# Router logits of a two-layer encoder trunk, made with the router's 36 columns stationary and turned back by two transposes

## The reference

```
g_logits = t @ w_group + b_group            # 256 tokens x 4 groups
e_logits = t @ w_expert + b_expert          # 256 tokens x 32 experts
p_group, g_sel = softmax(g_logits), argmax(g_logits)      # top 1 of 4 groups
top_v, top_i = top_k(e_logits of the chosen group, 2)     # top 2 of its 8 experts
gates = softmax(top_v) * p_group[g_sel], spread over the 32 experts
out = sum_e gates_e * (silu(t @ w1_e) * (t @ w3_e)) @ w2_e
```

## Time and profile before

| what | value |
|---|---|
| median of 3 runs | 1806.16 us |
| lowest, highest | 1806.05, 1807.55 us |
| profiled execution: first to last instruction (span) | 1807.0 us |
| mean granted TensorE clock of it | 0.953 |
| PE busy | 1640.9 us (91%) |
| PEld busy | 1163.6 us (64%) |
| DVE, ACT, POOL busy | 733.5 (41%), 414.5 (23%), 57.5 us (3%) |
| DMA | 543.77 MB, mean 301 GB/s |
| MATMUL psum_T<-router_w,xT | 128 records, 17.5 us busy |

### The profile page before, as it was taken

The page is one execution under the profiler, slowest core; times in us unless marked ns, Lnnn a source line. Parts: engine busy times, 40 slices in busy tenths (PEclk is TensorE's granted clock), DMA queues, the critical chain, the costliest instruction groups (busy, mean ns, idle before and its releaser), DMA issues.

```text
span 1807.0 us, 25442 instructions
## 1 busy us (share of the span) xinstructions
PE 1640.9 (91%) x9809; PEld 1163.6 (64%) x9809; DVE 733.5 (41%) x1154; ACT 414.5 (23%) x559; POOL 57.5 (3%) x82
## 2 busy tenths in 40 slices
PE   7999999998997998789789999999989887998785
PEld 7999998887552455345287988988855552455341
DVE  5545444443322232232264756757343222232233
ACT  5343343441000000000154334333310000000001
POOL 4010000100000000000011000000000000000000
PEclk9999999998999999999899999999989999999997
DMA  8545455457899999999944465464669999999996
GB/s 267 187 160 167 162 162 169 157 210 286 339 423 425 427 425 425 425 427 425 412 170 140 144 206 176 151 208 163 248 272 418 423 424 426 426 425 425 425 427 262
DMA packets 149418, 543.77 MB, mean 301 GB/s; under 512 B 8736, under 2 KB 25456, under 8 KB 116208
## 3 DMA queue, kind: packets, MB, share of 16 engines
q1 hardware_dynamic: 148448, 541.14, 77.0%
q0 software_dynamic: 912, 1.82, 0.4%
HBM read 540.83 MB, written 2.10 MB: 300 GB/s over the span
## 4 chain that ended last, share of the span: by engine, by line
PE 58%; issue 27%; DMA 9%; DVE 2%; ACT 1%; SPq 1%; DVEq 0%; POOLq 0%; POOL 0%; ACTq 0%
PE psum_G L662 33%; PE psum_S L662 16%; DMA ring<-in_moe_w 9%; PE psum_A L662 5%; PE psum_T L662 3%; DVE w_lo L406 1%; SPq L507 1%; ACT w_hi L402 1%; DMA x<-in_x 0%; PE psum_A L669 0%; DVE x L1580 0%; ACT squares L1122 0%; POOLq L598 0%; DVE h L1815 0%; PE psum_T L881 0%
## 5 line engine op out<-in xcount | busy, mean ns | idle before, releaser
L406 DVE TENSOR_TENSOR w_lo<-ring,w_hi 128x2048 fp32r<-128x2048 f32 x126 | 289.2, 2298 | 288.9 <-ACT w_hi L402 284.7
L662 PE MATMUL psum_A<-ring,arena 128*32 128x512 f32 x1984 | 272.8, 684 | 107.0 <-DMA ring<-in_moe_w 105.3
L402 ACT CAST w_hi<-ring 128x2048 fp32r<-128x2048 f32 x128 | 244.1, 1907 | 244.4 <-PE psum_G L662 155.9
L662 PEld LDWEIGHTS psum_A<-ring,arena 128*32 128x32 f32 x1984 | 65.1, 117 | 264.7 <-issue 264.6
L662 PE MATMUL psum_G<-arena_two,h 128*128 (+1 forms) x1024 | 230.8, 385 | 0.2
L662 PEld LDWEIGHTS psum_G<-arena_two,h 128*128 128x128 f32 x1024 | 225.8, 311 | 0.4 <-DVEq L1591 0.4
L1698 DVE COPY arena_two<-psum_A 128x512 f32<-128x512 f32 x64 | 44.3, 692 | 290.9 <-PE psum_A L662 290.5
L1728 DVE TENSOR_TENSOR x<-x,psum_S 128x512 f32<-128x512 f32 x128 | 88.1, 688 | 161.7 <-PE psum_S L662 161.7
L662 PE MATMUL psum_G<-xT_hi,w_hi 128*128 128x256 f32 x512 | 148.8, 291 | 0.9 <-DVE w_lo L406 0.6
L662 PE MATMUL psum_G<-xT_hi,w_lo 128*128 128x256 f32 x512 | 144.8, 283 | 0.0
L662 PE MATMUL psum_G<-xT_lo,w_hi 128*128 128x256 f32 x512 | 144.7, 283 | 0.0
(11 more groups left out here) (224 smaller groups left out, 2087.8 us busy)
## 6 DMA issues: line engine op xcount, KB each, us to landing
ring<-in_moe_w SPq DMA_DIRECT2D x376, 1024.0 KB, 17.2
ring<-in_sb_w_in SPq DMA_DIRECT2D x48, 1024.0 KB, 5.0
ring<-in_ml_w_in SPq DMA_DIRECT2D x48, 1024.0 KB, 5.1
ring<-in_sb_w_out SPq DMA_DIRECT2D x16, 1024.0 KB, 4.9
ring<-in_ml_w_out SPq DMA_DIRECT2D x16, 1024.0 KB, 5.0
extra_one<-in_moe_w SPq DMA_DIRECT2D x4, 1024.0 KB, 8.0
extra_two<-in_moe_w SPq DMA_DIRECT2D x4, 1024.0 KB, 13.6
x<-in_x SPq DMA_DIRECT2D x2, 1024.0 KB, 5.9
```

The costliest lines, as they stand in the source:

```text
L402: act.copy(w_hi[:, slot_place(j), :], ring[:, slot_place(j), :]).then_inc(hi_made, 1)
L406: dve.tensor_tensor(w_lo[:, slot_place(j), :], ring[:, slot_place(j), :], w_hi[:, slot_place(j), :].bitcast(F32), ALU.subtract).then_inc(l ...
L662: return pe.matmul(dst, lhsT, rhs, start=start, stop=stop, skip_group_check=True)
```

## The change

The operands of the logits' matmuls change places. For each tile k one f32 matmul takes the 36 columns of `router_w` as stationary operand and both token blocks of `xT`, 256 columns, as the moving one. The result is turned: 36 x 256 in T0, 36 logits on the partitions. Behind the last one PE waits until DVE has copied T0 to the new tile `logits_t` (a view of the arena) and then turns the two halves back with two transposes into bank T1, where it lies as it lay in T0 before. DVE's route starts with that copy, signals it, and waits for `filled["T1"]` instead of `filled["T0"]`. SP's two extra loads still wait for `filled["T0"]`. The table of bank uses counts one more use of T1 in each layer.

```diff
-        phase(("norm_ffn", layer), A=XC, T0=1)
+        phase(("norm_ffn", layer), A=XC, T0=1, T1=1)
...
+        logits_t = r(T)[0:ROUTER]
...
                     for k in range(4 * c, 4 * c + 4):
-                        for b in range(TB):
-
-                            last = mm(psum["T0"][:, b * ROUTER:(b + 1) * ROUTER], xT[:, k, b * P:(b + 1) * P],
-                                      router_w[:, k, :], k == 0 and b == 0, k == KT - 1)
+                        last = mm(psum["T0"][0:ROUTER, 0:T], router_w[:, k, :], xT[:, k, :], k == 0, k == KT - 1)
                     if c == XC - 1:
                         last.then_inc(filled["T0"], 1)
+                        pe.wait_ge(emptied["T0"], base["T0"] + 1)
+                        claim("T1", base["T1"])
+                        for b in range(TB):
+                            last = pe.transpose(psum["T1"][:, b * ROUTER:(b + 1) * ROUTER], logits_t[:, b * P:(b + 1) * P],
+                                                ident[0:ROUTER, 0:ROUTER])
+                        last.then_inc(filled["T1"], 1)
...
                 dve.wait_ge(filled["T0"], first_use["norm_ffn", layer]["T0"] + 1)
+                dve.tensor_copy(logits_t, psum["T0"][0:ROUTER, 0:T])
+                dve.drain().then_inc(emptied["T0"], 1)
+                dve.wait_ge(filled["T1"], first_use["norm_ffn", layer]["T1"] + 1)
                 for b in range(TB):
-                    last = dve.scalar_tensor_tensor(out=logits[:, b, :], in0=psum["T0"][:, b * ROUTER:(b + 1) * ROUTER],
+                    last = dve.scalar_tensor_tensor(out=logits[:, b, :], in0=psum["T1"][:, b * ROUTER:(b + 1) * ROUTER],
                                                     scalar=rstd[:, b:b + 1], in1=router_b[:, :],
                                                     op0=ALU.mult, op1=ALU.add)
-                last.then_inc(emptied["T0"], 1)
+                last.then_inc(emptied["T1"], 1)
```

## The result

The changed kernel takes 1809.59 us (median of 20 runs, 1808.7 to 1810.37) against 1807.24 us for the kernel before (20 runs on the same chip, 1805.9 to 1808.35). The ratio is 1.0013 [1.0007, 1.0019], or +2.35 us [1.3, 3.4]. The forecast was +2.5 us and 1808.7 us. So the sum came out, and it was no change by the mark of 0.2%. It came out by luck: three of its terms were mis-sized, and their errors cancel. That is what the rest is about.

The account below looks back on a forecast made before the run. PE bounds the out stages, the weight stream the experts, and the router's stretch delays that stream; +0.12 + 0.05 + 2.36 = +2.5 us on 1806.16 gives 1808.7 us, own range 1807.3 to 1809.9, 8 in 10 from 1805.4 to 1810.8.

Parts of the forecast that it names:

- The path: Between last logits matmul and mask, each lost microsecond restarts SP's weight stream a microsecond later, one for one, both layers.
- The logits steps inside the projection: Three steps a layer: half as many records, each twice as long, +0.02 us a step, +0.12 us for six.
- The rival that loads are not hidden: Every load in the logits steps stands between two matmuls: up to 0.114 us a record, 1816.0 us; chance 0.04.
- The fp32r pace: Rival: 256 f32 columns move as fast as fp32r ones, 0.115 us a logits record, 1800.6 us; chance 0.04.
- The rule of the Trainium skill that was weighed there: A load overlaps running matmuls only when its row group differs; the prediction said its trace disagrees.
- The last logits step: Step before the route, mostly at half clock: 3.61 us in layer 0, 2.75 in layer 1; +0.05 us for both.
- the rival that the clock holds: 256-column stream keeps PE at full clock in the last logits step: 1.89 us a layer, sum -0.7 us; chance 0.07.
- The handoff: After the last logits: DVE copy, drain, two half-clock transposes, return to DVE; 1.18 us a layer, 2.36 for both.
- its predicted lower bound of 0.87: Handoff with both transposes at full clock: 0.87 us a layer.
- The sum: +0.12 for steps inside the projection, +0.05 for last steps, +2.36 for handoffs: +2.5 us, 1808.7 us.
- The gap of 1.2 us to the bias: Sign: 1.2 us in place of 0.04 between the last logits matmul's end and DVE's first bias instruction.
- The restart of SP 1.2 to 1.4 us later in layer 0: Sign: mask, gather and SP's first issue of the next chunk come 1.2 to 1.4 us later than before.

Follow-up runs that it names:

- warm_route: Kernel before, plus unread 432-column f32 matmuls in PE's waits: one before the last turn, one before the last logits, seven before the count matmuls; 1805.43 us, ratio 0.9990.
- before_again: The kernel before, unchanged, run once more for a second profile; 1809.56 us.
- handoff_only: Kernel before with its old logits, plus only DVE's copy and PE's two transposes, their result unread; 1809.67 us, ratio 1.0013.
- grouped: Changed kernel with logits steps 0, 1 and 2 run together at the place of step 2; 1808.16 us, ratio 1.0007 of the kernel before.

## Why the prediction came out, and which of its steps failed

**The path.** Right. In layer 0 SP's queue restarts 21.2 us behind the count matmuls in all eleven profiles without unread matmuls (20.5 in warm_route, where they ran at a held clock). In layer 1 it is 21.2 us too, but 22.9 in before_again, handoff_only and grouped, where the first up projection was slow (below). The pause of 0 GB/s stays, and handoff_only shows two handoffs of 1.06 to 1.09 us as +2.35 us [0.7, 4.0] of time.

**The logits steps inside the projection, +0.02 us each.** This term was mis-sized. The pace was right: records 0.22 us apart, for 0.215 from the earlier trace rows. What was left out is the entry and the exit: with a narrow f32 operand the load is not taken ahead, and a step costs 0.25 to 0.27 us more. The earlier trace rows could not show it, since both of its operands have 128 columns. The last turn began 0.76 us later in layer 0, so six steps cost about +1.5 us, not +0.12. The rival that loads are not hidden was priced on each record and is wrong as such (there is no gap inside a step); it holds at the two ends of a step. The fp32r pace is refuted. Counting from the first logits record to the next projection matmul, as the earlier trace rows do, hides the entry; the count has to start at the last matmul ahead of it. The rule of the Trainium skill that was weighed there (TensorE: Matmul & The Clock Gate, section Packing small matmuls) fails here as well, as it was put there: loads for the same rows do overlap running matmuls, inside a step and, with 128 columns, at its start. The same section also has loads for a background weight buffer pulled ahead; these rows do not speak against that.

**The last logits step, +0.05 us for both layers.** Failed in size and in its reason. It takes 1.89 us in both layers: the rival that the clock holds, given 0.07, is what happened, to the hundredth of its 1.89. The argument against it was that in layer 0 the clock fell 0.07 us into the step, so the step had no say. That was a reading of one execution as if the place were fixed. Other executions of the same form fall 0.7 to 2.6 us into it, and the price of the old form is thereby an average: 2.4 us a step, not the 3.51 and 2.80 of the profile. Against 2.4 the new step gains 0.5 us a layer, about 1.0 us in all. So the rival had the step right and its own sum wrong: it set 1.89 against 3.61 and 2.75, and knew nothing of the entries and exits, and its -0.7 us did not come.

**The handoff, 1.18 us a layer.** Mis-sized by the same cause: 0.84 us, its predicted lower bound of 0.87, since the transposes run at full clock. At half clock handoff_only measured 1.06 to 1.09, with 0.12 us for its extra signal, so even there 1.18 was high, by the transposes: 0.43 us for the pair, not 0.64. These move 36 columns from 36 rows, those of the earlier trace rows 128 from 128; which of the two makes them shorter no run separates. Both layers: 1.7 us, not 2.36.

**The sum.** +1.5 for the steps, -1.0 for the last steps (a mean over few profiles), +1.7 for the handoff: +2.2 us, against +2.35 [1.3, 3.4] measured and +2.5 predicted. Errors of +1.4, -1.1 and -0.7 us cancelled. The base was off too. The profiled execution had the slowest last steps of the four profiles with that form, so its own counterpart after is only 0.7 us longer. The forecast's 1808.7 rests on the median of three runs, 1806.16; twenty runs of the same kernel gave 1807.24, and differ by 2.45 us among themselves, not by 0.8. And the lower end of the forecast's own range does not follow from what is said of it: the handoff at its lower bound gives 1806.16 + 0.17 + 1.74 = 1808.1, not 1807.3.

**What would show it.** 64 records, 0.22 us apart: right. Last steps of 3.6 and 2.75 us: wrong, 1.89. The gap of 1.2 us to the bias: from the end of the last logits matmul (425.57 + 1.89 = 427.46) to 428.46 it is 1.00, in which DVE first runs its rank instruction (L1599, 427.54); with the clock held the logits are ready about when DVE is. The restart of SP 1.2 to 1.4 us later in layer 0: wrong, 0.05 earlier; in layer 1 it is 0.74 later (1345.48 for 1344.74). The prediction said that it is wrong "if the clock's fall comes at another place than before in both layers"; that came true. The sum held for other reasons than those given.

**Still open.** Which property of the f32 narrow load keeps it from being taken ahead. And a scatter of some 1.7 us between executions: in some profiles the clock falls in layer 1's first up projection, as in before_again, where it is 0.54 from 1340 to 1342 us:

```profile
1340.12 5.33 PE L662 MATMUL psum_A<-ring,arena 128*32 128x512 f32 x32 [0.83 <-issue]
```

The up projection takes 5.33 us there, where it took 3.64 in the first profile; in grouped and handoff_only it was slow as well (5.29 and 5.33). It was seen in profiles and not provoked.

## What to carry to other kernels

Where the clock can fall on the path, a place in one trace is a sample: profile the same kernel a few times before a term rests on it, and ask what the new form of the work does to the clock, not only what it costs at the clock it finds. Count an inserted step from the last foreign matmul ahead of it to the second one behind it, since a change of operand shape is paid at the ends. And when an experiment changes a buffer's size, keep every other buffer's address, or check the GB/s of the stages that the edit should not touch.

## What the runs showed of the hardware beyond that

- The granted clock fell to 1.2 GHz under 48 records of f32 matmuls with 36 moving columns inside a projection, though PE and PEld were busy for 100% of the time (both layers of one execution); over 24 records of 256 moving columns at that place it stayed at 2.4 GHz. In the last step, behind two short waits of PE, it fell within 2.6 us in 8 of 8 layers with 36 moving columns and held in 13 of 14 with 256; with unread matmuls in PE's waits it held with 36 too, in both layers of warm_route.
- An f32 stationary operand of 36, 40 or 64 columns between 128-column ones costs 0.32 to 0.34 us a step more than one of 128 columns (2.51 us, 2.53 with 64 columns, against 2.19).
- 128 bytes of shift of the weight ring (with the tiles of x ahead of it) in SBUF: 416 against 423 GB/s in the same window, and 15 us of 1807.
- Unread matmuls that keep PE at work over the router's stretch pay for themselves: 0.9990 [0.9981, 0.9999], the upper end of which is close to 1.
